# A two-block transformer kernel on one core: the mixer's matmul units in another order, and scan rows and masks in fewer matmuls

## What is computed

```python
proj = h @ w_in                       # z 1024, xs 1024, B 256, C 256, dt 16, cq 384, ckv 256, k_rope 32
xBC = silu(causal_depthwise_conv(concat([xs, Bm, Cm]), conv_w, conv_b))      # width 4
dt = softplus(dt_raw + dt_bias);  A = -exp(a_log)
y = ssd_chunked(xh, dt, A, Bm, Cm) + d_skip * xh        # per head: exp(masked a_cum[t] - a_cum[s]) * (C B^T), times xdt
y_ssd = rmsnorm(y * silu(z), groups of 512)
q = rmsnorm(cq) @ w_uq;  kv = rmsnorm(ckv) @ w_ukv      # 8 heads: 64 + 32 rope, values of 128
y_mla = rmsnorm(causal_attention(q, k, v))
out = concat([y_ssd, y_mla]) @ w_out
```

## Time and profile before

| | us |
|---|---|
| median of 3 runs (1332.77 to 1336.35) | 1334.93 |
| the profiled execution | 1337.1 |
| its span, first to last instruction | 1335.5 |
| PE busy | 1247.7 (93%) |
| PE weight loads busy | 1126.3 (84%) |
| DVE busy | 841.2 (63%) |
| ACT busy | 586.6 (44%) |
| POOL busy | 68.2 (5%) |
| mean granted clock of PE | 0.971 |

### The profile page before, as it was taken

How to read it: one execution, slowest core, us unless ns; L and a number is a source line. 1 busy time by engine, 2 the same in 40 slices (tenths; PEclk the granted TensorE clock), 3 DMA queues, 4 the chain that set the end, 5 groups by cost and what they waited for, 6 DMA issues and landing times.

```text
span 1335.5 us, 20204 instructions
## 1 busy us (share of the span) xinstructions
PE 1247.7 (93%) x8065; PEld 1126.3 (84%) x8065; DVE 841.2 (63%) x1166; ACT 586.6 (44%) x759; POOL 68.2 (5%) x107
## 2 busy tenths in 40 slices
PE   6998999999999899999989999988797698999996
PEld 6886899999888689999979999977686687999995
DVE  4765587777766567877567544475486566544445
ACT  4444444444544454344454443445355444444332
POOL 8000011110000001110000000000000000000000
PEclk9998999999999999999989999989897899999998
DMA  6633398887353339887525655425341004455550
GB/s 227 205 106 115 127 346 298 299 292 263 132 167 117 123 114 355 299 296 238 189 95 168 211 188 188 159 85 177 126 154 68 0 32 158 167 184 186 188 205 32
DMA packets 140153, 236.39 MB, mean 177 GB/s; under 512 B 6341, under 2 KB 106934, under 8 KB 140086
## 3 DMA queue, kind: packets, MB, share of 16 engines
q1 hardware_dynamic: 127280, 196.95, 43.9%
q0 software_dynamic: 10400, 37.77, 8.0%
q10 hardware_dynamic: 2406, 0.74, 0.2%
HBM read 234.37 MB, written 1.05 MB: 176 GB/s over the span
## 4 chain that ended last, share of the span: by engine, by line
PE 77%; DVE 12%; ACT 6%; issue 3%; DMA 1%; ACTq 0%; DVEq 0%; SPq 0%
PE ps L1544 13%; PE ps L1546 12%; PE ps L1545 12%; PE ps L1607 10%; PE ps L1609 10%; PE ps L1611 10%; DVE wlo L895 3%; ACT whi L530 2%; PE ps L1571 1%; PE ps L1763 1%; PE ps L1631 1%; PE ps L1587 1%; DVE stage L975 1%; ACT work L622 1%; DVE mx L987 1%
## 5 line engine op out<-in xcount | busy, mean ns | idle before, releaser
L895 DVE TENSOR_TENSOR wlo<-raw,whi 128x2048 fp32r<-128x2048 f32 (+2 forms) x188 | 423.5, 2260 | 218.5 <-ACT whi L530 218.0
L530 ACT ACTIVATE whi<-raw 128x2048 fp32r<-128x2048 f32 (+2 forms) x188 | 353.9, 1889 | 272.7 <-PE ps L1611 183.3
L1544 PE MATMUL ps<-ah,whi 128*128 128x256 f32 x1392 | 400.6, 288 | 20.3 <-DVE wlo L895 13.4
L1545 PE MATMUL ps<-al,whi 128*128 128x256 f32 x1392 | 397.8, 286 | 0.0
L1546 PE MATMUL ps<-ah,wlo 128*128 128x256 f32 x1392 | 397.7, 286 | 0.0
L1544 PEld LDWEIGHTS ps<-ah,whi 128*128 128x128 f32 x1392 | 271.0, 195 | 26.1 <-issue 14.6
L1545 PEld LDWEIGHTS ps<-al,whi 128*128 128x128 f32 x1392 | 271.4, 195 | 1.8
L1546 PEld LDWEIGHTS ps<-ah,wlo 128*128 128x128 f32 x1392 | 271.0, 195 | 0.0
L1607 PE MATMUL ps<-whi,hh 128*128 128x512 f32 x424 | 133.4, 396 | 0.0
L1609 PE MATMUL ps<-wlo,hh 128*128 128x512 f32 x424 | 131.7, 392 | 0.0
L1611 PE MATMUL ps<-whi,hl 128*128 128x512 f32 x424 | 131.1, 391 | 0.0
(11 more groups left out here) (350 smaller groups left out, 1637.0 us busy)
## 6 DMA issues: line engine op xcount, KB each, us to landing
stage<-in_w_ada_dram POOLq DMA_DIRECT2D x72, 512.0 KB, 6.5
raw<-in_w_up_dram SPq DMA_DIRECT2D x32, 1024.0 KB, 6.4
raw<-in_w_down_dram SPq DMA_DIRECT2D x32, 1024.0 KB, 6.8
raw<-in_ffn_w_gate_dram SPq DMA_DIRECT2D x22, 1024.0 KB, 5.2
raw<-in_ffn_w_up_dram SPq DMA_DIRECT2D x22, 1024.0 KB, 5.2
raw<-in_ffn_w_down_dram SPq DMA_DIRECT2D x22, 1024.0 KB, 4.8
raw<-in_moba_w_qkv_dram SPq DMA_DIRECT2D x12, 1024.0 KB, 6.4
raw<-in_w_in_dram SPq DMA_DIRECT2D x10, 1024.0 KB, 5.3
```

What stands on the lines that cost most here:

```text
L530: A.activation(whi[:, s, 0:size], raw[:, s, 0:size], ACT.Copy).then_inc(w_hi, 1)
L895: V.tensor_tensor(wlo[:, s, 0:size], raw[:, s, 0:size], whi[:, s, 0:size].bitcast(F32), ALU.subtract).then_inc(w_lo, 1)
L1544: T.matmul(o, wmh, xh[:, c], start=(c == 0), stop=False)
L1545: T.matmul(o, wmh, xl[:, c], start=False, stop=False)
```

## The change

It does these things:

- **Order of units.** After the tail come xs/B/C unit 0, 1, (latent transposes), 2, the two `w_uq` units, then xs/B/C 3, `w_ukv` 0, 4, `w_ukv` 1, 5, transposes of xs, then the z units with the k transposes, the q transposes and the first two scores between them. SP loads in that order.
- **z units** are 4 k-tiles by 512 columns instead of 2 by 1024, two banks each: 6 and 7 for the first half of z, 4 and 5 for the second. The second half is copied raw by DVE during attention (`z_raw`) and gets its Silu after the scan's last exponential.
- **Banks.** Everything wide of the latent path uses 0 to 3; xs/B/C units use 4, 5, 6, 4, 5, 4; attention values and scan results go to 6, 7 (first half of heads) and 4, 5 (second half).
- **ACT and DVE lists** weave conv taps, Silu, splits and copies of different units; the rope angles (16 memsets and 14 small DVE instructions, one Sin on ACT) move into the SwiGLU layer before.
- **After attention.** C B^T and the gate's rows go ahead of the norm; the norm's squares are taken by halves; ACT scales one half of the result, DVE the other; writing the result out as high and low parts is woven into heads 1 to 4 of the scan, and half of the sum with xs and z into heads 10 and 12.
- **Fewer matmuls.** `decay_rows` issues two instead of six; `pair_score` and `mla_score` three instead of four.
- **Splits.** Output units 1 and 2 are split inside the latent attention (heads 1 and 5), units 3 and 4 after the scan.

```diff
-U_Z = U_TAIL + 4
-U_UQ = U_Z + 4
-U_UKV = U_UQ + 2
-U_XBC = U_UKV + 2
-U_OUT = U_XBC + 6
+U_X = [U_TAIL + k for k in (4, 5, 6, 9, 11, 13)]
+U_UQ = U_TAIL + 7
+U_KV = [U_TAIL + 10, U_TAIL + 12]
+U_Z = U_TAIL + 14
+U_OUT = U_Z + 4
...
+X_BANK = [4, 5, 6, 4, 5, 4]
+MLA_BANK = [4, 5, 2, 3]
...
             def pair_score(h):
                 o = bank(h % 2, SEG)
                 T.matmul(o[:, 0:P], q[:, 0:P], k[:, 0:P], start=True, stop=False)
-                T.matmul(o[:, 0:P], identr[:], maskq[:], start=False, stop=True)
-                T.matmul(o[:, P:SEG], q[:, P:S], k, start=True, stop=False)
-                return T.matmul(o[:, S:SEG], identr[:], maskq[:], start=False, stop=True)
+                T.matmul(o[:, P:SEG], q[:, P:S], k, start=False, stop=False)
+                return masked(o)
+            def masked(o):
+                return T.matmul(outer_blocks(o), identr[:], maskq[:].unsqueeze(1).to_broadcast([P, 2, P]), start=False,
+                                stop=True)
...
             def decay_rows(h):
                 if h >= 2:
                     pe.wait_ge(dec_exp, h - 1)
                 o = bank(h % 2, SEG)
-                sel = identr[:, h:h + 1].to_broadcast([P, P])
-                T.matmul(o[:, 0:S], sel, rowh[:], start=True, stop=False)
-                T.matmul(o[:, 0:S], sel, rowl[:], start=False, stop=False)
-                T.matmul(o[:, 0:P], identr[:], maskt[:], start=False, stop=True)
-                T.matmul(o[:, S:SEG], sel, rowh[:, P:S], start=True, stop=False)
-                T.matmul(o[:, S:SEG], sel, rowl[:, P:S], start=False, stop=False)
-                T.matmul(o[:, S:SEG], identr[:], maskt[:], start=False, stop=True).then_inc(row_ps, 1)
+                T.matmul(o, selr[:, h:h + 1].to_broadcast([P, P]), rowc[:], start=True, stop=False)
+                T.matmul(outer_blocks(o), identr[:], maskt[:].unsqueeze(1).to_broadcast([P, 2, P]), start=False,
+                         stop=True).then_inc(row_ps, 1)
...
# the list of PE
+            x_unit(0)
+            x_unit(1)
             transposes(xn, [(lat_done, 1)] * TT, [0, 1, 2], 5)
-            pe.wait_ge(z_done, 1)
+            x_unit(2)
             pe.wait_ge(in_ready, PAIR0["lat"] + 3)
...
+            z_unit(0)
+            pe.wait_ge(xs_tok, 1)
+            pe.wait_ge(xs_tok2, 1)
+            pe.wait_ge(krope_done, 1)
+            heads_T(ktok)
+            z_unit(1)
             pe.wait_ge(qtok_done, 1)
+            pe.wait_ge(mqk_copied2, 1)
+            heads_T(qtok)
+            z_unit(2)
             pe.wait_ge(mqk_copied, 1)
+            for h in range(2):
+                mla_score(h).then_inc(scored, 1)
+            z_unit(3)
+            mla_heads(2 * H)
...
# the list of DVE, latent attention
+            def mla_heads(h0, scale):
+                for h in range(HM):
                     dve.wait_ge(scored, h0 + h + 1)
                     head_max(h0 + h, h, bank(h % 2, SEG), scale)
+                    if h == 1:
+                        splits(U_OUT + 1)
+                        dve.wait_ge(w_used, U_Z + 4)
+                        V.tensor_copy(z[:, :, 512:D], ps[:, 4:6]).then_inc(z_raw, 1)
+                    if h == 3:
+                        gate_diag(1, mix_diag)
+                    if h == 5:
+                        splits(U_OUT + 2)
```

More of the change, by code:

```diff
@@ L789, in _ @@
             ins.then_inc(lat_sq, 1)
+            splits(U_X[2])
             act.wait_ge(sp_in, 2)
@@ L845, in _ @@
-            ins.then_inc(mla_sq, 1)
-            gained("mla", bh, col(vA, COL_A, "mla_norm_w_2"))
+            conv_silu(0)
+            splits(U_X[3])
+            conv_tap0(2)
+            conv_silu(1)
+            splits(U_KV[0])
+            act.wait_ge(w_used, U_UQ + 2)
+            A.activation(qtok[:, 0], banks(0, 768), ACT.Copy).then_inc(mq_tok, 1)
+            splits(U_X[4])
+            conv_silu(2)
+            conv_tap0(3)
+            splits(U_KV[1])
+            kv_copy(0)
+            splits(U_X[5])
@@ new lines, in _ @@
+            conv_silu(3)
+            conv_tap0(4)
+            splits(U_Z)
+            kv_copy(1)
+            splits(U_Z + 1)
+            conv_silu(4)
+            conv_tap0(5)
+            splits(U_Z + 2)
+            act.wait_ge(xs_T, 1)
+            act.wait_ge(krope_done, 1)
+            A.activation(xs[:, 0], banks(0, D), ACT.Copy).then_inc(xs_tok, 1)
+            conv_silu(5)
+            splits(U_Z + 3)
+            act.wait_ge(w_used, U_Z + 2)
+            A.activation(z[:, :, 0:512], ps[:, 6:8], ACT.Silu).then_inc(z_done, 1)
@@ new lines, in _ @@
+            act.wait_ge(mqk_T, 2)
+            for b in range(4):
+                ins = A.activation(qTm[0:QK, 2 * b:2 * b + 2], ps[0:QK, b].rearrange("p (h n) -> p h n", h=2), ACT.Copy)
+            ins.then_inc(mqk_copied, 1)
+            splits(U_OUT)
+            mla_heads(2 * H, QK ** -0.5)
+            for half in range(2):
+                if half:
+                    act.wait_ge(mla_sq, 1)
+                for t in range(TT):
+                    act.wait_ge(o_ready, 2 * half + t + 1)
+                    ins = A.activation(sq_scratch[:, t], xn[:, t, 512 * half:512 * half + 512], ACT.Square,
+                                       accum_out=sums[:, 2 * half + t:2 * half + t + 1])
+                ins.then_inc(mla_sq, 1)
@@ new lines, in _ @@
+            link(V.scalar_tensor_tensor(sm[:, 5], sm[:, 0], 0.0, sm[:, 4], ALU.max, ALU.add))
+            dve.wait_ge(al_exp, 1)
+            V.scalar_tensor_tensor(by_t(sm[:, 6]), by_t(sm[:, 5]), -1.0,
+                                   aexp[:].unsqueeze(1).to_broadcast([P, TT, H]), ALU.mult, ALU.mult).then_inc(ssd_in, 1)
+            dve.wait_ge(qtok_done, 1)
+            u1, u2 = tail[:, :, KR0:KR0 + 16], tail[:, :, KR0 + 16:KR0 + 32]
+            r4 = [rope[:, k, 0:32].rearrange("p (t j) -> p t j", t=TT) for k in range(4)]
@@ new lines, in _ @@
+            conv_taps(5)
+            splits(U_Z + 2)
+            dve.wait_ge(xs_T, 1)
+            dve.wait_ge(krope_done, 1)
+            V.tensor_copy(xs[:, 1], banks(2, D)).then_inc(xs_tok2, 1)
+            splits(U_Z + 3)
+            dve.wait_ge(mqk_T, 1)
+            for b in range(4):
+                ins = V.tensor_copy(kTm[b // 2][0:QK, 2 * (b % 2):2 * (b % 2) + 2],
+                                    ps[0:QK, b].rearrange("p (h n) -> p h n", h=2))
+            ins.then_inc(mqk_copied2, 1)
```

463 lines of the change are left out of this document (254 added, 209 removed).

## The result

The changed kernel takes 1294.6 us (median of 5 runs, 1289.3 to 1309.4), the kernel before 1334.3 in the same session (1331.9 to 1336.4); the ratio is 0.9693, 95% interval 0.9676 to 0.9711 (the run of 1309.4 us, at a lower clock than the other four, is left out of the ratio). The forecast was 1300, range 1289 to 1316: held, and 5 us too high.

What follows compares the result with a forecast made beforehand. PE, busy 93% of the span, was taken as the bound. Terms -29.9 + 2.0 + 5.0 - 7.0 - 1.0 - 1.4 - 2.8 = -35.1 against the profiled 1337.1 gave 1302.0, so a median of 1300; range 1289 to 1316.

Steps and rivals of the forecast that it cites:

- First stretch: Tail units to first weights transpose: 82.8 us instead of 112.7, -29.9, with +2.0 added for half a further gap.
- the walk: Hand-timed PE, ACT and DVE lists of the first stretch: one PE gap, 1.5 us, before the transposes of k.
- rival 2: Clock stays up and chains overlap better, in the first stretch and after: 1291 us; chance 0.13.
- Latent attention: First weights transpose to last values: 21.2 us instead of 16.2, +5.0, with 4.7 us idle from output unit 2's split.
- Attention to scan: Between latent attention and scan, 19.3 us before: -7.0, as C B^T and the gate's rows run in the gap.
- 3.7 us at half clock again: Attention to scan: the transposes after the norm's scaling take 3.7 us at half clock; first exponential at 12.3 us.
- Scan: Scan, 22.0 us before: fewer matmuls save 4.8 us, extra work in heads adds 1.9 and 1.8; net -1.0.
- Output units: After the scan's transposes: the 1.40 us wait for the split goes, since unit 4 is split ahead; -1.4.
- Masks of the first two attentions: One mask matmul fewer in twenty woven heads bound by PE, 0.14 us each: -2.8.
- Angles: Rope angles in the SwiGLU layer before, 3 us of DVE between splits: put at nothing.
- rival 1: DVE becomes the bound of the first stretch; 14 hand-overs at 1 us, about 1314 us; chance 0.18.
- Rival 3: PE falls to the lower clock level through the first stretch: 1366 us if all of it; chance 0.03.

Runs made afterwards that it cites:

- the second: Second profile of the changed kernel, the same program profiled again unchanged: 1291.5 us in its profiled execution; median of that repeat 1291.0 us.
- the first profile: First profile of the changed kernel; it caught the longest of the five runs, 1309.4 us.
- the extra work: Changed kernel with an extra DVE subtraction of 512 columns ahead of each of 14 splits in the first stretch: 1297.7 us, ratio 0.9723.
- the neighbour that lost it every time: Changed kernel with the first w_ukv unit moved ahead of the fourth xs/B/C unit, directly behind w_uq: 1315.8 us, ratio 0.9865.
- the identity transposes: Changed kernel with w_ukv 0 directly behind w_uq, plus 20 identity transposes on PE in its wait before the norm's transposes: 1313.8 us, ratio 0.9847.
- three others: Changed kernel with output unit 2's split behind the scan: median 1290.4 us; plus 20 identity transposes: 1287.6; plus gain pairs in heads 1, 3, 5, 7: 1287.3.
- neighbours of it (nine of nine in two): Changed kernel with w_ukv 0 directly behind w_uq: 1315.8 us; the same plus 20 identity transposes before the norm's transposes: 1313.8 us.

## Why the prediction came out as it did

From the spans of the profiles, the second against before: 45.9 us; the medians of that session give 42.6 and those of the first 39.7. I had 35.1. Nearly all terms erred to the same side: five stretches gained 10.5 us more than their terms say, and the masks at least 2.2 less. Against the profile the sum is 10.8 us short, against the medians 5 to 8. Each term as the prediction put it:

- **First stretch: right, its additions were not needed.** Work 79.3 forecast, 79.39 measured. One gap at the place named, before the transposes of k, 0.81 us for 1.5. DVE's rows there are the walk's (taps, split, copy of xs), which ran 0.2 to 0.5 us ahead of it:

```profile
955.48 2.67 DVE L1126 SCALAR_TENSOR_TENSOR work<-ps,vB,work 128x255 f32<-128x255 f32 x6
958.07 2.28 DVE L957 TENSOR_TENSOR wlo<-raw,whi 128x2048 fp32r<-128x2048 f32 x1
960.27 1.22 DVE L1554 COPY stage<-ps 128x1024 f32<-128x1024 f32 x1
```

  The 2.0 us of half clock and half of a further gap (2.0) did not come: the clock is 1.00. -32.5 instead of -27.9. The wait of 0.81 us, behind 58 us of work, did not lower the level; rival 2 was right in this. The releaser of that gap is shown as "issue" and not as DVE's copy, as I had written; the copy ends at 961.5, when PE starts.
- **Latent attention: mechanism right, sizes a little high.** +3.3 for +5.0. The split's gap is 3.84 for 4.7, ended by an exponential as said, and its removal took it away; the wait for the copy of z is 0.51 for 1.5, that of the last heads 0.55 for 1.2.
- **Attention to scan: right but for the clock.** 10.2 us, for 12.3 with half clock and 10.5 without; the gap is 3.13 for 4, ended by the scaling. What fell is the step "3.7 us at half clock again". In the first profile that step was true: 3.65 us, and 12.1 us from the last values to the first exponential. Which of the two it would be was luck.
- **Scan: mis-sized on both sides.** -2.8 for -1.0. A head without extra work takes 0.98 us for 1.05. Heads 1 to 4 take 1.35, not 1.5: DVE's multiplication and its two extra instructions are the whole of the period, ACT's are hidden beside them. The two later heads cost 0.8 and 0.3 us, not 0.9 each.
- **Output units: -1.7 for -1.4,** no wait at the fifth unit.
- **Masks of the first two attentions: wrong.** -2.8 forecast, at most -0.6 measured: the stretches of woven heads are 0.29 and 0.35 us shorter (95.09 for 95.38, 81.47 for 81.82). The step that failed is "the first mask matmul takes PE 0.14 us until the next": with it gone, the product before it takes 0.22 us in place of 0.14, so here a matmul's distance to the next depended on what followed it. And "twenty woven heads are bound by PE" is wrong at their end, where DVE is waited for. The estimate from the Trainium skill, page "TensorE: Matmul & The Clock Gate", section "LDWEIGHTS (loading the stationary operand)", was 0.107 us a removed matmul; the rows show 0.06.
- **Angles: nothing, as said.** From the transposes of that layer's input to the first tail unit 207.2 us, before 207.6.
- **Ahead of the first stretch** the two profiles differ by 2.9 us, which looks like the 2.8 of the masks and is not: the masks are 0.6 and the angles' layer 0.4 of it, and most of the rest is clock in the attentions, which differs from execution to execution (from 125 to 130 us it was 0.50 before and 0.68 after; the tail units begin between 881.0 and 886.9 us in kernels that are the same until there).

The chances: rival 1 (DVE the bound) did not come, but the price of the extra work says how near it was: of 8.7 us more, 6.9 showed. Rival 3, the lower level, came in one run of ten, and not in the stretch where I looked for it but in the scan, where 21.1 us at full clock had seemed safe. The Trainium skill, page "TensorE: Matmul & The Clock Gate", section "A second HAM failure mode: psum-queue depth-cycling", which I cited for it, tells of a clock that is lost and regained again and again while matmul groups cycle through banks; in the scans of the long runs the profiles show a single fall that lasts through the rest of the scan (36 us at 0.50 in the first profile), and ended in the first output unit.

## What to carry to other kernels

Where a result must leave the banks before the next unit, look at what stands in front of the copy in its engine's list: 0.95 us of copy made a wait of 5.78, and a whole unit of other work in its place, in other banks, took out 32 us of one stretch. Before taking matmuls out of a loop that PE alone fills, ask what keeps its clock: fewer matmuls gained 3 to 6 us in the kernel that mostly kept its level and cost 8 to 9 in the neighbour that lost it every time. And run such a kernel ten times and not three, since two programs with one median may have different worst runs.

## What the runs showed of the hardware

- PE stayed at the lower level through stretches of 25 to 30 us in which it was never idle (30.00 busy of 30.00 at 0.50), a row, mask and product loop of 1.8 us a head in place of 0.98. In all four profiles that show it the full level came back within the first output unit, with matmuls of 512 columns. It had been my assumption that a level returns a few microseconds after the wait that lowered it, as after 959.49 in the earlier trace rows; in two other profiles it did so inside the same kind of loop, in its third head. What makes the difference is open.
- The level fell where PE's last wait over 1.2 us was long past: behind the identity transposes it fell at 1023.5 us, in the third head of the scan, and the last such wait (3.83 us) had ended at 1004.4.
- The loss was a matter of chance in one program (one run of ten; two of six in three others) and came every time in neighbours of it (nine of nine in two).
- A removed matmul gave back less than its distance to the next: 0.06 of 0.14 us.
